# An mLSTM layer's C q for four-token samples, computed with q instead of C as the stationary operand

## The reference

```python
def step(carry, xs):
    C, n, m = carry                       # C: (8 samples, 128 v, 128 d)
    inter = bc + m[..., None]
    mt = jnp.maximum(inter, dmc)
    wi = jnp.exp(inter - mt)
    p = jnp.exp(dc - mt[..., None]) * qkc
    num = (wi[..., None] * jnp.einsum('bhvd,bhld->bhlv', C, qc)
           + jnp.einsum('bhls,bhsv->bhlv', p, vc))
    den = wi * jnp.einsum('bhd,bhld->bhl', n, qc) + jnp.sum(p, axis=-1)
    h = num / jnp.maximum(jnp.abs(den), jnp.exp(-mt))[..., None]
```

## Time and profile before

| | |
|---|---|
| median of 3 runs | 2030.31 us (2029.37 to 2030.98) |
| the profiled execution's own time | 2027.79 us |
| its span, first to last instruction | 2025.6 us |
| TensorE busy | 1952.9 us, 96% of the span |
| TensorE weight loads | 1896.6 us, 94% |
| VectorE busy | 1209.8 us, 60% |
| ScalarE busy | 936.3 us, 46% |
| GpSimd busy | 200.2 us, 10% |
| mean granted TensorE clock | 0.991 of 2.4 GHz |

### The profile page before, as it was taken

The page is one execution under the profiler, slowest core; times in us unless marked ns, Lnnn a source line. Parts: engine busy times, 40 slices in busy tenths (PEclk is TensorE's granted clock), DMA queues, the critical chain, the costliest instruction groups (busy, mean ns, idle before and its releaser), DMA issues.

```text
span 2025.6 us, 39152 instructions
## 1 busy us (share of the span) xinstructions
PE 1952.9 (96%) x14427; PEld 1896.6 (94%) x14427; DVE 1209.8 (60%) x2417; ACT 936.3 (46%) x1846; POOL 200.2 (10%) x311
## 2 busy tenths in 40 slices
PE   6899999999999999999999999999999999999997
PEld 4789999999999999999989999999999999999996
DVE  3756656666664555546655566764466764466753
ACT  4434444454444444445554454443354443444533
POOL 4102111211110010110012100000000000000032
PEclk9999999999999999999999999999999999999999
DMA  7444545455445756655557566666556666566551
GB/s 164 115 114 133 148 128 149 133 133 140 136 131 153 186 151 169 170 144 160 178 148 198 136 161 164 166 166 166 166 156 162 161 160 168 167 166 167 155 146 64
DMA packets 566395, 307.87 MB, mean 152 GB/s; under 512 B 6379, under 2 KB 561475, under 8 KB 565971
## 3 DMA queue, kind: packets, MB, share of 16 engines
q1 hardware_dynamic: 523691, 278.22, 51.0%
q10 hardware_dynamic: 42400, 27.88, 4.8%
q0 software_dynamic: 192, 0.26, 0.2%
HBM read 293.32 MB, written 13.02 MB: 151 GB/s over the span
## 4 chain that ended last, share of the span: by engine, by line
PE 79%; DVE 7%; ACT 5%; issue 5%; POOL 2%; DMA 1%; ACTq 1%; DVEq 0%; POOLq 0%; SPq 0%
PE products L1689 23%; PE products L1691 22%; PE products L1690 22%; DVE w_lo L521 2%; ACT w_hi L514 2%; PE mixer L1669 2%; PE products L1669 1%; POOL sig L629 1%; PE mixer L1770 1%; PE mixer L1776 1%; PE mixer L1777 1%; PE mixer L1885 1%; DVE conv_out L1347 1%; DVE u_gate L1604 1%; DVE u_val L1604 1%
## 5 line engine op out<-in xcount | busy, mean ns | idle before, releaser
L521 DVE TENSOR_TENSOR w_lo<-w_raw,w_hi 128x512 fp32r<-128x512 f32 x1037 | 722.6, 710 | 706.5 <-ACT w_hi L514 703.8
L514 ACT ACTIVATE w_hi<-w_raw 128x512 fp32r<-128x512 f32 x1037 | 632.4, 627 | 664.9 <-PE products L1691 632.1
L1689 PE MATMUL products<-h_hi,w_hi 128*128 128x288 f32 x1536 | 481.1, 313 | 7.4 <-DVE w_lo L521 5.4
L1691 PE MATMUL products<-h_hi,w_lo 128*128 128x288 f32 x1536 | 458.1, 298 | 0.0
L1690 PE MATMUL products<-h_lo,w_hi 128*128 128x288 f32 x1536 | 457.9, 298 | 0.0
L1689 PE MATMUL products<-f_hi,w_hi 128*128 128x288 f32 x1408 | 418.4, 297 | 1.0 <-ACT r L1106 1.0
L1691 PE MATMUL products<-f_hi,w_lo 128*128 128x288 f32 x1408 | 418.0, 297 | 0.0
L1690 PE MATMUL products<-f_lo,w_hi 128*128 128x288 f32 x1408 | 414.7, 295 | 0.0
L1689 PEld LDWEIGHTS products<-h_hi,w_hi 128*128 128x128 f32 x1536 | 293.1, 191 | 22.8 <-DVE w_lo L521 11.3
L1690 PEld LDWEIGHTS products<-h_lo,w_hi 128*128 128x128 f32 x1536 | 293.0, 191 | 0.5
L1691 PEld LDWEIGHTS products<-h_hi,w_lo 128*128 128x128 f32 x1536 | 291.5, 190 | 0.0
(11 more groups left out here) (431 smaller groups left out, 2348.4 us busy)
## 6 DMA issues: line engine op xcount, KB each, us to landing
w_raw<-in_w_in SPq DMA_DIRECT2D x96, 1024.0 KB, 6.0
w_raw<-in_w_up SPq DMA_DIRECT2D x88, 1024.0 KB, 5.9
w_raw<-in_w_down SPq DMA_DIRECT2D x32, 1024.0 KB, 5.9
w_raw<-in_w_out SPq DMA_DIRECT2D x16, 1024.0 KB, 7.8
w_raw<-in_w_down SPq DMA_DIRECT2D x16, 768.0 KB, 4.9
w_raw<-in_w_branch_a SPq DMA_DIRECT2D x8, 1024.0 KB, 5.4
w_raw<-in_w_branch_b SPq DMA_DIRECT2D x8, 1024.0 KB, 5.3
S_sample<-in_state_gdn_S ACTq DMA_DIRECT2D x8, 512.0 KB, 4.2
```

What stands on the lines that cost most here:

```text
L514: nc.scalar.activation(ring_slot(whi, whi2, n, ring), raw[:, s % slots, 4 * j:4 * j + 4], ACT.Copy).then_inc(hi_ready, 1)
L521: nc.vector.tensor_tensor(ring_slot(wlo, wlo2, n, ring), raw[:, s % slots, 4 * j:4 * j + 4], ring_slot(whi, whi2, n, ring).bitcast(F32), A ...
L1689: mm(out, w_hi, x_hi, start=start, stop=False)
L1691: return mm(out, w_lo, x_hi, start=False, stop=stop)
```

## The change

C q is computed the other way round: for each sample, `qws[:, b]` is stationary (128 x 32: q of the four tokens in their own columns, zeros in the other 28), and the sample's whole `cts[:, b]` (128 x 128) moves. The output of sample b has 32 rows and goes to partitions 32 (b mod 4) to 32 (b mod 4) + 31 of `pm[:, 2, 0:P]`; samples 4 to 7 are added on top of samples 0 to 3, in whose rows they hold zeros. ScalarE copies the 128 x 128 result to `cq4`, and one matmul with the constant `tok4` (1 where row mod 32 is the token) adds the four groups of rows and turns them into the numerator's layout. All eight samples stand in local slot 4, behind the denominator's two matmuls, which move ahead of them; the numerator's matmul of v and the closing one stand in local slot 6. ScalarE takes the denominator in local slot 5 in place of 6. `cq4` lies in the memory of `cts` (samples 2 on), `km` in that of samples 0 and 1 as before. GpSimd makes `tok4` at the start with five instructions; VectorE zeroes `qws` once.

```diff
+        tok4 = mx.put("token_of_row", [P, TS])
-        qw, prd = s8.put("qw", [P, TS]), s8.put("qw_n", [P, TS])
+        qws, prd = s8.put("qw_of_seq", [P, NB, TS]), s8.put("qw_n", [P, TS])
+        cq4 = nc.alloc_sbuf_tensor_at("cq_parts", [P, P], F32, offset=cts_at + 2 * P * 4)
+        def own(t):
+            ap = t[:]
+            return bass.AP(tensor=ap.tensor, offset=ap.offset, ap=[ap.ap[0], [TS + L, NB], [1, L]])
@@ gpsimd, constants
+            done(pool.memset(tok4[:], 0.0))
+            for r in range(P // TS):
+                keep(tok4[:], [[-1, TS]], -TS * r, 1, 1.0, ALU.not_equal)
@@ scalar, mlstm
-                yield 6
-                act.wait_ge(*mt.after("so", i))
+                yield 5
+                act.wait_ge(*mt.after("den", i))
                 act.wait_ge(*md_.before(i))
                 nc.scalar.activation(dn[:], pm[:, 1, 0:T], ACT.Abs).then_inc(*ma.done("abs"))
+                act.wait_ge(*mt.after("cq", i))
+                nc.scalar.activation(cq4[:], pm[:, 2, 0:P], ACT.Copy).then_inc(*ma.done("cq"))
@@ vector
+                nc.vector.memset(qws[:], 0.0).then_inc(qws_zero, 1)
-                d("qw", tt(qw[:], q_t[:, TP:T], mrow[:, 2 * T:2 * T + TS], ALU.mult))
+                d("qw", tt(own(qws), in_seq(q_t[:, TP:T]), in_seq(mrow[:, 2 * T:2 * T + TS]), ALU.mult))
@@ tensor, mlstm
                 yield 4
+                pe.wait_ge(*md_.after("prs", i))
+                mm(pm[:, 1, TP:T], ones[:], prd[:], start=True, stop=False)
+                mm(pm[:, 1, TP:T], ones[0:TS], mpt[0:TS, TP + P:], start=False, stop=True).then_inc(*mt.done("den"))
                 pe.wait_ge(*ma.after("ct1", i))
-                pe.wait_ge(*md_.after("prs", i))
+                for b in range(NB):
+                    r = b % 4 * TS
+                    last = mm(pm[r:r + TS, 2, 0:P], qws[:, b], cts[:, b], start=b < 4, stop=b >= 4)
+                last.then_inc(*mt.done("cq"))
+                yield 6
+                pe.wait_ge(*ma.after("cq", i))
                 mm(pm[:, 0, TP:T], vt[0:TS, 2, 0:P], mpt[0:TS, TP + P:], start=True, stop=False)
-                for b in range(NB):
-                    if b == NB // 2:
-                        yield 5
-                    cc = slice(b * L, b * L + L)
-                    mm(pm[:, 0, TP + b * L:TP + (b + 1) * L], cts[:, b], qw[:, cc], start=False, stop=b == NB - 1)
-                mm(pm[:, 1, TP:T], ones[:], prd[:], start=True, stop=False)
-                mm(pm[:, 1, TP:T], ones[0:TS], mpt[0:TS, TP + P:], start=False, stop=True).then_inc(*mt.done("so"))
+                mm(pm[:, 0, TP:T], cq4[:], tok4[:], start=False, stop=True).then_inc(*mt.done("so"))
```

More of the change, by code:

```diff
@@ L116, in build @@
     CHUNKS = [4, 4, 3]
-    N_CONST = 5 + 4 * 2 - 1 + 4 * 6 + 3 + 1 + 9 + 5
+    N_CONST = 5 + 4 * 2 - 1 + 4 * 6 + 3 + 1 + 9 + 5 + 5
     N_STORED, N_GROW, N_LROW = 4, 2 * H, 2 * H + 2 * sum(CHUNKS) + 4
@@ L329, in build @@
         scan_t = Steps(sem("scan_pe"), "T0 u0 k1 T1 ksS u1 trS TS oS nrm Ss1 Ss2")
-        ma = Steps(sem("mlstm_act"), "d1 d2 kw0 kw1 kw2 v0 ct0 ct1 so1 so2 so3 abs cp hi")
+        ma = Steps(sem("mlstm_act"), "d1 d2 kw0 kw1 kw2 v0 ct0 ct1 so1 so2 so3 abs cq cp hi")
         md_ = Steps(sem("mlstm_dve"), "so D0 D0b D1 Ds pt1 pt2 qw prs C0 np ns ns2 mx rc h ho cs1 cs2 cs3 cs4 lo")
         mp = Steps(sem("mlstm_pool"), "kv4 km cs")
-        mt = Steps(sem("mlstm_pe"), "ktr vtr kq ct0 ct1 num ns so cp C")
+        mt = Steps(sem("mlstm_pe"), "ktr vtr kq ct0 ct1 num ns den cq so cp C")
         gate_a = Steps(sem("gates_act"), "expA abs exp ln beta eG er4 er wi emt fw sw")
@@ L343, in build @@
         br_a = Steps(sem("branch_act"), "sa0 sa1 sb0 sb1 hi0 hi1 sa2 sa3 sb2 sb3 hi2 hi3")
-        vt_ones, uu_zero = sem("vt_ones_set"), sem("u_pads_zero")
+        vt_ones, qws_zero, uu_zero = sem("vt_ones_set"), sem("qw_of_seq_zero"), sem("u_pads_zero")
         br_d = Steps(sem("branch_dve"), "s0 s1 lo0 lo1 s2 s3 lo2 lo3")
@@ L1482, in mlstm @@
                 yield 2
-                d("qw", tt(qw[:], q_t[:, TP:T], mrow[:, 2 * T:2 * T + TS], ALU.mult))
+                dve.wait_ge(qws_zero, 1)
+                in_seq = lambda ap: ap.rearrange("p (b s) -> p b s", s=L)
+                d("qw", tt(own(qws), in_seq(q_t[:, TP:T]), in_seq(mrow[:, 2 * T:2 * T + TS]), ALU.mult))
                 step(md_, "qw", i)
-                d("prs", tt(prd[:].rearrange("p (b s) -> p b s", s=L), qw[:].rearrange("p (b s) -> p b s", s=L),
-                            n_s[:, :, i:i + 1].to_broadcast([P, NB, L]), ALU.mult))
+                d("prs", tt(in_seq(prd[:]), own(qws), n_s[:, :, i:i + 1].to_broadcast([P, NB, L]), ALU.mult))
                 yield 4
```

## The result

| | before | changed |
|---|---|---|
| median (lowest to highest) | 2030.31 us (2028.39 to 2031.4, 5 runs) | 2020.98 us (2016.39 to 2021.68, 5 runs) |
| ratio | | 0.995, 95% interval 0.9936 to 0.9965 |
| profiled execution, its span | 2027.79, 2025.6 us | 2020.98, 2019.3 us |

The kernel is faster by 9.3 us. The forecast was 2022.8 us, and the median lies 0.02 us under the low end of its range. On two more chips, the changed kernel gave 0.995 (0.9935 to 0.9965) and 0.9949 (0.9935 to 0.9962) of the kernel before: 8.7 and 9.5 us.

The account below looks back on a forecast made before the run. PE was taken to bound the mLSTM heads' stretch; two stops a head falling from 2.97 to 2.03 us save 7.5 us over eight heads, so 2030.3 - 7.5 = 2022.8 us, range 2021.0 to 2027.5.

Parts of the forecast that it names:

- The bound: mLSTM heads' stretch: PE is the bound, so a head's saving counts eight times, one to one.
- The stops of before: Two breaks per head in PE's products for the lane's own matmuls: 1.41 and 1.56, together 2.97 us.
- The group of eight: C q's eight matmuls, 16 passes in the first stop: four column groups at once, four rounds of 0.11, 0.44 us.
- First stop 1.31: Changed kernel's stop with the denominator's pairs, the samples' matmuls, tiling change and restart: 1.31 us a head.
- Second stop 0.72: Changed kernel's stop with v's matmul pair 0.33, closing matmul 0.22, 0.09 before and restart 0.08: 0.72 us a head.
- ACT in time, by some tenths: ACT's copy for the second stop done at most 1.68 us behind slot 4's last product, PE there at 1.7; late: 0.05.
- POOL covered: POOL's `km` (0.61 us) and scaling of C (1.90) start later but finish before they are needed; cost nothing.
- Pairs: Rival: strict issue order makes nine rounds of four, 0.55 us a head more, 2027.2 us; with similar partial overlap 0.12.
- Groups not at once: Rival: column groups don't overlap, loads hidden; 0.29 us a head slower, +2.3 us, 2032.6; chance 0.08.
- Loads serialized: Rival: each column group's load waits for the matmul before; group 2.24 us, +5.9 us, 2036.2; chance 0.05.
- The sum of the stops: Both stops from 2.97 to 2.03 us, 0.94 less a head, 7.5 us for eight heads.
- the stagger: First stop's term for column groups starting up to 0.09 us apart if their loads of 0.03 come one by one.

Follow-up runs that it names:

- one_group: The changed kernel with all eight samples on the same 32 columns of the array, closing matmul and copy on 32 rows: 2029.96 us, 0.9996 of the kernel before.
- stop_early: The changed kernel with its second stop one slot earlier, in local slot 5 instead of 6: 2030.28 us, 1.0 of the kernel before.
- pair_order: The changed kernel with the samples' matmuls issued in the order 0 4 1 5 2 6 3 7: 2022.09 us, 0.9959 of the kernel before.
- again: The changed kernel, same program, run on a second chip: 2020.62 us, 0.995 of the kernel before.
- after_2: The changed kernel, same program, run a third time on another chip: 2021.27 us, 0.9949 of the kernel before.
- num_first: The changed kernel with the numerator's matmul of v moved from the second stop to the first, run twice: 2017.17 and 2019.22 us.
- gdn_groups: The same operand exchange also in the DeltaNet heads, atop the changed kernel with a one-matmul denominator and v's matmul in local slot 3: 2018.71 us, 0.9942 of before.
- folded: The changed kernel with one matmul for the denominator (VectorE adds the decay rows) and v's matmul in local slot 3, run twice: 2019.22 and 2017.78 us.
- old_grouped: The kernel before, C q in its old form, with denominator, v's matmul and samples in one stop in local slot 4, run twice: 2035.35 and 2033.3 us.

## Why the prediction was right, and where it was wrong

- **The bound.** Right. PE is busy in all of the heads' stretch, before and after, and a stop's saving comes back one to one: 8.0 us in the stops, 8.10 in the stretch. "What is saved here isn't waited for again later" was right for waits, and left out that the clock can change with the program.
- **The stops of before.** 2.97 us forecast from one head; 2.984 over all eight.
- **The group of eight.** Four rounds of 0.11 by analogy with the row groups: right, and carried by one_group (1.93 against 0.65 us). The four rounds start within 0.35 and take 0.46 us; in one_group the same passes take 1.77, so four groups gave 3.8 times. The estimate from the Trainium skill (TensorE: Matmul & The Clock Gate, Part 3), by its 2.38 times for three groups, was 0.6; the trace decides.
- **First stop 1.31.** Measured 1.244. The term "the groups start up to 0.09 apart" isn't there: they start 0.02 apart, so the loads of 32 columns overlap one another too. The denominator's pair was 0.02 dearer than the 0.21 that was taken.
- **Second stop 0.72.** Measured 0.745; the closing matmul's part was 0.25 where 0.22 was taken.
- **ACT in time, by some tenths.** Right: no wait, with 0.11 to 0.33 us to spare. stop_early shows what the slot between bought, 1.32 us a head.
- **POOL covered.** Right as to time; `km` got slower (below).
- **The rivals.** *Pairs* was tested by pair_order and fails (0.02 us). *Groups not at once* was priced rightly for the stretch (2.3; 2.25) and did not happen. *Loads serialized* fails, and with it the Trainium skill's rule (TensorE: Matmul & The Clock Gate, Part 3) that a load overlaps running matmuls only where the row group differs: in one_group and in the change all loads are on the same 128 rows, and start every 0.11 us, or four at once, under running passes. The trace disagrees with the rule taken literally.
- **The sum of the stops.** 7.5 us forecast, 8.0 measured: mis-sized by 0.05 a head. The first stop is 0.07 shorter than forecast, as much as the stagger was too large; the stops of before add 0.01, and the second stop takes 0.02 back. With 8.0 the same reckoning gives 2022.3 us, inside the range.
- **The step that failed** is the last one, "The median of the runs lies 2.5 above it, so the predicted time is 2030.3 - 7.5", and the low end put on it, "The range starts at 2021.0, where the stagger and part of the changes cost nothing (0.2 a head)". Both take everything outside the stops for unchanged, and the range holds the stops as its one unknown (0.2 a head from 2022.8 would even be 2021.2). The medians moved by 9.3, 8.7 and 9.5 us on three chips, for the same 8.0 in the stops. What stands in the place of "unchanged": 0.5 us less outside the span in every execution, and a granted clock that differs, by an estimated 1.9 us in the mean of the executions on record. The stage of `w_out` alone differed by 1.7 to 2.0 us between executions of one program, through half clock behind a wait that the earlier trace rows hide in a mean of 0.99 over 988 us. How the first comparison's 9.3 splits can't be told, since the clocks of the kernel before are not on record there. That the median fell outside by 0.02 us and not inside is chance; that the gain is larger than the stops' 8.0 is not chance alone. The effect was right, and the ends should have been set by it and by 2 to 3 us of such scatter besides.

## What to carry to other kernels

Where a float32 matmul moves a few columns past a 128-column stationary operand, its load sets the cost; exchange the operands, pad the small one to 32 columns, spread the independent products over the four column groups, and the group took about a quarter of the time here, if one later matmul can add the parts and the copy between fits behind other work (one slot of products too early cost all of it here). When two kernels differ by tenths of a per cent, cut both traces by events and compare stages, then read the granted clock behind each long wait: a wait of 3.6 us cost 3.6 us and 1.5 to 5.3 more.

## What had not been expected of the hardware

- **Passes on free column groups overtake.** pair_order's 1.264 against 1.244 us: the order in the program of passes for different column groups hardly matters, four rounds are made of it either way.
- **Half clock behind a short wait, by different lengths.** Around the end of the wait of 3.6 us the granted clock fell to 1.2 GHz, and for how long went with when it fell, in all fourteen profiles: for 3.4 us where it fell from 0.1 us before to 0.6 after the end of the wait (before, again, after_2, one_group, both num_first), for 6.8 where it fell 1.2 or 1.4 after it (the changed kernel's first profile, pair_order), and for 10.2 to 13.7 where it fell 1.1 to 1.5 before it, with PE still idle (stop_early, gdn_groups, both folded, both old_grouped). It cost some 1.7 us for each 3.4 inside the stage. Without the wait there was none. By stretch (columns as above), the changed kernel's first profile, where the wait ends at 1018.71, and folded, where it ends at 1013.55:

```profile
1019.94:1026.76 6.82, 6.82 (x28) 5.22 (x28) 2.17 (x4) 2.70 (x6) 0.00 (x0) 0.50 0.15 42
```

```profile
1012.12:1022.36 10.24, 8.81 (x34) 7.22 (x35) 4.50 (x8) 5.32 (x11) 0.00 (x0) 0.50 0.10 25
```

- **Half clock without a wait, and behind a wait of 1.25 us.** In old_grouped_2 it fell twice in or just behind stops in which PE was busy all the time, with passes of 4 and 32 columns; in stop_early it fell once behind a wait of 1.25 us, and not behind seven more like it.
- **`km` on POOL and `w_lo` on DVE get in each other's way.** The same 128 x 256 product of two tiles, against the earlier trace rows, in all heads before and changed (min/median/max ns, first and last start):

```profile
L695 POOL TENSOR_TENSOR kw_by_seq<-kw,seq_of_pair x8: 613/613/613, 687.7 to 905.8; 128x256 f32<-128x256 f32 x8
```

```profile
L707 POOL TENSOR_TENSOR kw_by_seq<-kw,seq_of_pair x8: 612/1167/1167, 688.3 to 899.3; 128x256 f32<-128x256 f32 x8
```

It starts behind the second stop, which now lies in another slot, and there DVE starts a `w_lo` within 0.02 us of it, in all eight heads; before, no DVE operation ran beside it. Heads 1 and 6 of the changed kernel, counted from 0:

```profile
718.47 0.69 DVE L529 TENSOR_TENSOR w_lo<-w_raw,w_hi 128x512 fp32r<-128x512 f32 x1 [0.90 <-ACT w_hi L522]
718.47 1.17 POOL L707 TENSOR_TENSOR kw_by_seq<-kw,seq_of_pair 128x256 f32<-128x256 f32 x1 [26.33 <-PE mixer L1906]
869.16 1.15 DVE L529 TENSOR_TENSOR w_lo<-w_raw,w_hi 128x512 fp32r<-128x512 f32 x1 [0.91 <-ACT w_hi L522]
869.15 0.61 POOL L707 TENSOR_TENSOR kw_by_seq<-kw,seq_of_pair 128x256 f32<-128x256 f32 x1 [26.29 <-PE mixer L1906]
```

In six heads `km` takes 1.17 us and `w_lo` its usual 0.69; in the last two `km` takes 0.61 and `w_lo` 1.13 and 1.15. One of the two keeps its time and the other takes about 0.5 us more. PE loses nothing by it: its stop for the matmuls that read `km` is 0.84 us in both kernels.
